# The value projection's first four slabs take ring places behind the down-projection's; the activation sum and the last norm's scales move

## The reference

```python
def swiglu(x, w_in, w_out):
    gate, up = jnp.split(x @ w_in, 2, axis=-1)
    return (jax.nn.silu(gate) * up) @ w_out
...
        h = layer_norm(DEEPNORM_ALPHA * h + y, ln_g[i, 0], ln_b[i, 0])
        h = layer_norm(DEEPNORM_ALPHA * h + swiglu(h, ffn_w_in[i], ffn_w_out[i]), ln_g[i, 1], ln_b[i, 1])
```

## Time and profile before

| | |
|---|---|
| median of 3 runs | 1138.2 us (1135.93 to 1138.34) |
| the profiled execution, its own time | 1138.06 us |
| its span, first to last instruction | 1136.2 us |
| mean granted TensorE clock | 0.997 |
| PE busy | 1122.7 us (99%) |
| DVE busy | 787.8 us (69%) |
| ACT busy | 570.1 us (50%) |
| POOL busy | 317.3 us (28%) |

### The profile page before, as it was taken

How to read it: one execution, slowest core, us unless ns; L and a number is a source line. 1 busy time by engine, 2 the same in 40 slices (tenths; PEclk the granted TensorE clock), 3 DMA queues, 4 the chain that set the end, 5 groups by cost and what they waited for, 6 DMA issues and landing times.

```text
span 1136.2 us, 18410 instructions
## 1 busy us (share of the span) xinstructions
PE 1122.7 (99%) x6828; PEld 996.3 (88%) x6828; DVE 787.8 (69%) x1266; ACT 570.1 (50%) x926; POOL 317.3 (28%) x212
## 2 busy tenths in 40 slices
PE   9999999999999999999999999999999999999997
PEld 7888888989999999888787877778989999997886
DVE  5070163798888885997603776766888888868987
ACT  4345144245555555556324665672435555556553
POOL 1538425141222212000155343551322222230001
PEclk9999999999999999999999999999999999999999
DMA  6433214076897755664232212142159879727551
GB/s 226 171 144 111 111 38 148 28 260 173 267 281 204 252 165 208 209 212 158 93 111 74 89 51 93 47 149 74 38 182 283 238 245 281 212 74 296 189 190 75
DMA packets 34459, 183.35 MB, mean 161 GB/s; under 512 B 3152, under 2 KB 7376, under 8 KB 20704
## 3 DMA queue, kind: packets, MB, share of 16 engines
q1 hardware_dynamic: 19472, 122.27, 29.9%
q0 software_dynamic: 8448, 46.14, 15.7%
q10 hardware_dynamic: 6480, 14.17, 3.5%
HBM read 180.46 MB, written 51.38 MB: 204 GB/s over the span
## 4 chain that ended last, share of the span: by engine, by line
PE 91%; DVE 3%; issue 2%; DMA 2%; ACT 1%; SPq 0%; DVEq 0%; POOL 0%; POOLq 0%; ACTq 0%
PE bank L2047 27%; PE bank L2049 27%; PE bank L2048 27%; PE bank L2499 2%; DVE s_w_lo L1321 2%; PE bank L2483 2%; DMA s_more_raw<-down 1%; PE bank L2130 1%; PE bank L2078 1%; PE bank L2520 1%; PE bank L2519 1%; DMA s_raw<-stream 1%; PE bank L2328 1%; PE bank L2321 0%; PE bank L2336 0%
## 5 line engine op out<-in xcount | busy, mean ns | idle before, releaser
L2047 PE MATMUL bank<-s_t_hi,s_w_hi 128*128 128x256 f32 (+1 forms) x832 | 264.4, 318 | 0.0
L2049 PE MATMUL bank<-s_t_hi,s_w_lo 128*128 128x256 f32 (+1 forms) x832 | 262.8, 316 | 0.0
L2048 PE MATMUL bank<-s_t_lo,s_w_hi 128*128 128x256 f32 (+1 forms) x832 | 262.8, 316 | 0.0
L1180 POOL TENSOR_TENSOR s_w_lo<-s_raw,s_w_hi 128x1024 fp32r<-128x1024 f32 x64 | 160.0, 2513 | 181.1 <-ACT s_w_hi L640 181.1
L640 ACT ACTIVATE s_w_hi<-s_raw 128x1024 fp32r<-128x1024 f32 x110 | 113.7, 1053 | 112.0 <-PE bank L2049 88.0
L2049 PEld LDWEIGHTS bank<-s_t_hi,s_w_lo 128*128 128x128 f32 x832 | 158.6, 191 | 10.2
L2047 PEld LDWEIGHTS bank<-s_t_hi,s_w_hi 128*128 128x128 f32 x832 | 158.7, 191 | 9.6 <-issue 0.2
L2048 PEld LDWEIGHTS bank<-s_t_lo,s_w_hi 128*128 128x128 f32 x832 | 158.7, 191 | 9.4
L1213 POOL TENSOR_TENSOR s_w_lo<-s_raw,s_w_hi 128x512 fp32r<-128x512 f32 x36 | 67.1, 1865 | 276.6 <-ACT s_w_hi L769 276.6
L2047 PE MATMUL bank<-s_t_hi,s_w_s_hi 128*128 128x256 f32 x432 | 122.4, 283 | 0.0
L2049 PE MATMUL bank<-s_t_hi,s_w_s_lo 128*128 128x256 f32 x432 | 122.2, 283 | 0.0
(11 more groups left out here) (248 smaller groups left out, 2483.3 us busy)
## 6 DMA issues: line engine op xcount, KB each, us to landing
s_raw<-stream SPq DMA_DIRECT2D x73, 1024.0 KB, 4.8
sums<-down POOLq DMA_DIRECT2D x12, 2816.0 KB, 20.9
sums<-sums POOLq DMA_DIRECT2D x4, 2816.0 KB, 13.2
s_more_raw<-sums SPq DMA_DIRECT2D x11, 1024.0 KB, 4.9
s_raw<-down SPq DMA_DIRECT2D x8, 1024.0 KB, 5.0
s_raw<-sums SPq DMA_DIRECT2D x5, 1024.0 KB, 4.9
s_ln_gb<-ln_gb ACTq DMA_DIRECT2D x4, 1024.0 KB, 7.1
s_more_raw<-down SPq DMA_DIRECT2D x4, 1024.0 KB, 6.9
```

The lines of the kernel that those rows point to most:

```text
L1180: nc.gpsimd.tensor_tensor(lo, raw_pair(SLOTS[place // 2])[:, n % 2, cols], hi.bitcast(F32), ALU.subtract).then_inc(lo_done, new)
L2047: nc.tensor.matmul(out, l_hi, r_hi, start=start, stop=False, skip_group_check=skip)
L2048: nc.tensor.matmul(out, l_hi, r_lo, start=False, stop=False, skip_group_check=skip)
L2049: return nc.tensor.matmul(out, l_lo, r_hi, start=False, stop=stop, skip_group_check=skip)
```

## The change

V0 to V3 leave the list of early slabs: they have no places of their own, are loaded and split behind the down-projection's slabs 36 to 39, and go to the ring places of these. Down-projection slabs 36 to 38 of the first layer load into `more_raw`, V0 to V3 into `raw`. The high halves of V0 and V1 stand on ACT between `turned_high(1)` and `square(2)`, those of V2 and V3 between `square(2)` and `square(3)`. The low halves of V0 and V1 are made by DVE, behind `turned_low(1)` and ahead of `centre(2)`; those of V2 and V3 by POOL, between the roots of tile 2 and tile 3. In the first layer `turned_low(1)` moves behind the means of tile 2.

In both layers `operand_sum(f, 2)` moves behind `low(8)`. In both the four merges of product 5 go tile by tile. In the last norm `scale` of tile 1 moves behind `centre` of tile 2, which gets a buffer of its own (`last_centred`), and the first term of the last mean moves behind the means of tile 2. `roots` is split into calls of `root`.

```diff
-EARLY = [FFN_IN[0], RPA_V, FFN_IN[1]]
+EARLY = [FFN_IN[0], FFN_IN[1]]
...
         early_places = {FFN_IN[0]: [(24, 28), (32, 36), (8, 12), (16, 20)],
-                        RPA_V: [(4, 12), (16, 20), (28, 32), (36, 40)],
                         FFN_IN[1]: [(32, 36), (40, 44), (76, 80), (68, 72)]}
...
         centred = sb_at("centred", [P, D_MODEL], F32, prod_at)
+
+        last_centred = sb_at("last_centred", [P, D_MODEL], F32, region)
...
                 if f is None:
-                    if slot >= RAWS:
-                        sp.wait_ge(slab_done, FFN_OUT[0])
                     sp.dma_start(raw_pair(slot), a["stream"][pair]).then_inc(raw_full[slot], 16)
                     continue
...
                 if early_of(n) is not None:
                     if n < RPA_V:
                         act.wait_ge(inter_done, TILES - 1)
-                    elif n < RPA_KQ:
-                        act.wait_ge(op_lo[0], lo_parts_until(PRODUCTS - 1, 1))
                     else:
...
                     if s == 35:
                         square(ln, 1)
                     split_hi(n0 + s)
-                if ln == 1:
-                    for j in range(TAIL):
-                        split_hi(n0 + DOWN + j)
                 for s in range(DOWN - TAIL, LAST_SLAB + 1):
                     split_hi(n0 + s)
                 if ln == 3:
@@ -731,7 +725,11 @@
                     return
                 turned_high(ln, 0, banks)
                 turned_high(ln, 1, banks)
+                split_hi(RPA_V)
+                split_hi(RPA_V + 1)
                 square(ln, 2)
+                split_hi(RPA_V + 2)
+                split_hi(RPA_V + 3)
                 square(ln, 3)
                 turned_high(ln, 2, banks)
                 turned_high(ln, 3, banks)
...
             feed_forward(0, FFN_IN[0])
-            roots(1)
+            root(1, 0)
+            root(1, 1)
+            root(1, 2)
+            pool.wait_ge(lo_done, RPA_V + 2)
+            for n in range(RPA_V + 2, RPA_V + TAIL):
+                split_lo(n)
+            root(1, 3)
             for n in range(RPA_V, RPA_KQ):
                 split_lo(n + RING)
...
-            def centre(ln, t):
+            def centred_of(ln, t):
+                return last_centred if (ln, t) == (3, 2) else centred
+
+            def centre(ln, t, behind=0):
 
                 if t == 0:
                     dve.wait_ge(gb_full, 16 * (ln + 1))
                 else:
-                    dve.wait_ge(normed[ln], t)
-                own(nc.vector.scalar_tensor_tensor(out=centred[:, :], in0=h[:, t, :], scalar=mean[:, t:t + 1],
+                    dve.wait_ge(normed[ln], t - behind)
+                own(nc.vector.scalar_tensor_tensor(out=centred_of(ln, t)[:, :], in0=h[:, t, :], scalar=mean[:, t:t + 1],
...
-                    nc.vector.scalar_tensor_tensor(out=h[:, t, cols], in0=centred[:, cols], scalar=rstd[:, t:t + 1],
+                    nc.vector.scalar_tensor_tensor(out=h[:, t, cols], in0=centred_of(ln, t)[:, cols], scalar=rstd[:, t:t + 1],
...
                 low(5)
                 operand_low(f, 1, 1)
                 low(6)
-                operand_sum(f, 2)
                 low(7)
                 low(8)
+                operand_sum(f, 2)
                 wait_product(dve, f, 0)
                 for t in early:
                     merge(f, 0, t, 0, first=True, minus=True)
...
                 scale(ln, 0)
                 low(35)
                 centre(ln, 1)
-                if ln == 1:
-                    for j in range(TAIL):
-                        split_low(n0 + DOWN + j)
                 for s in range(DOWN - TAIL, LAST_SLAB + 1):
                     low(s)
-                scale(ln, 1)
                 wait_product(dve, f, 5)
+                if ln == 1:
+                    scale(ln, 1)
                 for t in late:
                     merge(f, 5, t, 0, first=True, minus=True)
-                for t in late:
                     merge(f, 5, t, 1, last=True)
                 if ln == 1:
+                    dve.wait_ge(lo_done, RPA_V)
                     turned_low(ln, 0, banks)
-                    turned_low(ln, 1, banks)
                 dve.wait_ge(merged[f], 14)
-                if ln == 3:
-                    t = TILES - 1
-                    own(nc.vector.tensor_scalar(first_term[:, :], half_sum[:, t, 1:2], -ROOT_D / D_MODEL, ROOT_EPS,
-                                                ALU.mult, ALU.add))
                 dve.wait_ge(acc_done, TILES * (ln + 1))
                 merge(f, 6, 2, 0, last=True)
                 dve.wait_ge(merged[f], 15)
                 means(ln, 2)
-                centre(ln, 2)
-                scale(ln, 2)
-                dve.wait_ge(slab_done, n0 + DOWN)
                 t = TILES - 1
-                merge(f, 6, t, 0, last=True)
-                dve.wait_ge(merged[f], 16)
                 if ln == 1:
+                    turned_low(ln, 1, banks)
+                    split_low(RPA_V)
+                    split_low(RPA_V + 1)
+                    centre(ln, 2)
+                    scale(ln, 2)
+                    dve.wait_ge(slab_done, n0 + DOWN)
+                    merge(f, 6, t, 0, last=True)
+                    dve.wait_ge(merged[f], 16)
                     means(ln, t)
                     centre(ln, t)
                     scale(ln, t)
                     turned_low(ln, 2, banks)
                     turned_low(ln, 3, banks)
                     return
+                own(nc.vector.tensor_scalar(first_term[:, :], half_sum[:, t, 1:2], -ROOT_D / D_MODEL, ROOT_EPS,
+                                            ALU.mult, ALU.add))
+                centre(ln, 2, 1)
+                scale(ln, 1)
+                scale(ln, 2)
+                dve.wait_ge(slab_done, n0 + DOWN)
+                merge(f, 6, t, 0, last=True)
+                dve.wait_ge(merged[f], 16)
                 nc.vector.tensor_scalar(neg_mean[:, t:t + 1], half_sum[:, t, 0:1], -ROOT_D / D_MODEL, first_term[:, 0:1],
                                         ALU.mult, ALU.add).then_inc(mean_done, 1)
                 own(nc.vector.tensor_scalar(mean[:, t:t + 1], half_sum[:, t, 0:1], half_sum[:, t, 1:2], 1.0 / D_MODEL,
```

More of the change, by code:

```diff
@@ L1180, in split_lo, with root @@
                 nc.gpsimd.tensor_tensor(lo, raw_pair(SLOTS[place // 2])[:, n % 2, cols], hi.bitcast(F32), ALU.subtract).then_inc(lo_done, new)
+            def root(ln, t):
+                pool.wait_ge(squares, TILES * ln + t + 1)
+                if ln == 3 and t == TILES - 1:
+                    nc.gpsimd.tensor_tensor(rstd[:, t:t + 1], variance[:, t:t + 1], minus_half[:, 0:1], ALU.pow).then_inc(rstd_done, 1)
+                    return
+                own(nc.gpsimd.tensor_scalar(var_eps[:, t:t + 1], variance[:, t:t + 1], LN_EPS, None, ALU.add))
+                nc.gpsimd.tensor_tensor(rstd[:, t:t + 1], var_eps[:, t:t + 1], minus_half[:, 0:1], ALU.pow).then_inc(rstd_done, 1)
             def roots(ln):
                 for t in range(TILES):
-                    pool.wait_ge(squares, TILES * ln + t + 1)
-                    if ln == 3 and t == TILES - 1:
-                        nc.gpsimd.tensor_tensor(rstd[:, t:t + 1], variance[:, t:t + 1], minus_half[:, 0:1], ALU.pow).then_inc(rstd_done, 1)
-                        continue
-                    own(nc.gpsimd.tensor_scalar(var_eps[:, t:t + 1], variance[:, t:t + 1], LN_EPS, None, ALU.add))
-                    nc.gpsimd.tensor_tensor(rstd[:, t:t + 1], var_eps[:, t:t + 1], minus_half[:, 0:1], ALU.pow).then_inc(rstd_done, 1)
+                    root(ln, t)
             def out_projection(n0, ln):
```

## The result

| | before | after |
|---|---|---|
| median of 5 runs | 1138.01 us (1135.93 to 1138.34) | 1142.23 us (1142.01 to 1143.12) |
| span of the profiled execution | 1136.2 us | 1140.5 us |
| mean granted TensorE clock | 0.997 | 0.998 |
| PE's waits for lows: total, times, longest | 3.6, 3, 2.7 us | 4.2, 5, 1.4 us |

The changed kernel takes 1.0045 times as long, with a 95% interval of 1.0033 to 1.0057: slower, by 4.2 us. The forecast was 1142.5.

What follows compares the result with a forecast made beforehand. PE was taken as busy nearly throughout, losing time only in gaps, low clock or tail. Sum +4.4, ring places -0.4 and last norm +0.45 gave +4.4 on 1138.06: 1142.5 us, range 1138.0 to 1145.0.

Steps and rivals of the forecast that it cites:

- its four parts: Whole kernel: 2.2 in each layer's down-projection for the sum's move, -0.4 for the ring places, +0.45 for the last norm.
- Step 1, the sum: Both down-projections: the late sum holds operand_high(2) and split_hi(9) behind it; stops at slabs 9, 10, 12; +2.2 each, +4.4.
- the two old stops: PE's waits at slab 7, some 0.3 in the first layer's down-projection, 0.65 in the second's; -1.0 if they go.
- Step 2, the ring places: First layer's down-projection to tile 3's turn: long stop and low clock go, -4.65, but new stops leave only -0.4.
- the exclusion: VectorE operations with two SBUF inputs and GpSimd ones reading SBUF wait for each other's whole instruction, delaying scales, centres and roots.
- The terms for the tiles: New PE stops after the first layer's down-projection: 0.6 at V0, 1.4 at tile 2, 2.2 at tile 3.
- The undisturbed -3.7: Ring places by undisturbed durations: tile 3 turns at 558.2 against 561.92, -3.7 for the step.
- Step 3, the last norm: Last norm: root 2 is caught by centre(2), then scale(1); last merge at 1129.8, +0.45; without the exclusion -0.1.
- Undisturbed scales: Rival at 552 to 558: VectorE's scales don't wait for GpSimd; total +0.6, 1138.7 us; chance 0.18.
- a free sum: Rival: split_hi(9) isn't late or the sum's place doesn't hold it; -1.0 there, 1137.1 or 1133.2 us; chance 0.12.
- The clock didn't fall again: Rival: the clock falls in a new stop (1.4, 2.2 or 1.55), 1.75 each; 1144.2 or 1146 us; chance 0.15.
- the 1.75 of the prediction: Low clock (0.52) after the first layer's long down-projection stop: 1.75 of the 4.65 us lost there.

Runs made afterwards that it cites:

- the run with slab 9 first: Changed kernel, but ACT makes slab 9's high half before operand_high(2), the sum staying in its new place: 1138.04 us, 1.0002 times before.
- the last experiment: Kernel before with the sum between low(7) and low(8) and ACT's split of slab 9 ahead of operand_high(2): 1137.18 us, 0.9988 times before.
- the second set of edits: Four edits on the changed kernel: lows later on POOL 1146.82 us, last norm as before 1141.72, three repairs 1135.87, these with sum between low(7) and low(8) 1134.5.
- the three repairs: Changed kernel with slab 9 split before operand_high(2), lows of V2 and V3 on DVE, last norm as before: 1135.87 us, 0.9986 times before.

## Why the prediction was right

The sum was +4.4 and its four parts came out at +2.18, -0.83, +2.27 and +0.67, together 4.29. That the total is nearer than its parts is in part luck: the ring places gained 0.43 more than predicted, the last norm lost 0.22 more.

**Step 1, the sum.** Predicted 2.2 in each layer; the parts of the span are 2.18 and 2.27, the places of the stops alone 2.26 and 2.03. It is shown twice: taken back alone it gives 4.3, made alone it costs as much (4.6 between medians, 4.7 between spans, with a stop of 1.61 where the changed kernel has 1.40). The place of the loss was right too. By the starts the new stops were 1.52 and 1.67, 0.87 and 0.86, and 0.37 twice, where 1.55, 0.8 and 0.35 were worked out; the third, at slab 12, is too small for the list. The step that carried the forecast was to look at what stands behind `operand_high(2)` in ACT's queue; the run with slab 9 first shows that this queue, and not DVE's 3 us, held PE. One remark failed: that with slab 9 in time the two old stops would go as well (-1.0). 4.2 came back and not 5.2: small stops of 0.6 to 0.8 a layer stayed at slabs 10 and 12, which come from DVE's order behind the sum, and they weigh as much as the old ones. With the sum between low(7) and low(8) they are all but gone in the first layer: tile 0 turns 0.64 sooner (537.82 against 538.46).

**Step 2, the ring places.** Predicted -0.4, measured -0.83, and the same distance between the turns, 22.74 or 22.75, in the four kernels that have it in this form. The mechanism is shown: the exclusion was read off for other operations, and it holds for `scale` and `centre`, with 3.32 and 2.32 against 1.28. The rule of the Trainium skill (SBUF — State Buffer, Who interferes with whom) that whoever is issued first keeps the port to its end agrees with these rows, down to the order V2, `scale(2)`, V3, `centre(3)`. The terms for the tiles were too large: stops of 0.6, 1.4 and 2.2 were worked out; by the starts they were 0.7, 1.2 and 1.8 (the list has 0.43, 0.95 and 1.61). I had taken a low on POOL at 2.6, half of a pair of 5.23 that had itself been held up; alone it takes 2.40, a pair 4.67. The undisturbed -3.7 would have needed POOL's lows to run beside DVE for nothing; with the lows on DVE the turns are 20.61 apart instead of 23.57, a gain of 3.0. All these gains are against a profiled execution of the kernel before in which the clock fell (1.75). Where it didn't fall, the same ring places would lose some 0.9; that is an estimate, 1.75 - 0.83.

**Step 3, the last norm.** Predicted +0.45, measured +0.67. The exclusion is there, and what the order costs is 0.42, as worked out. The rest is the wait of 0.30 in front of `centre(2)`: from the merge's end at 1128.52 to `centre(2)` at 1129.38 it is 0.86, where the prediction had an estimate of 0.6 for the two means and the first term. Without that wait the same three take 0.60. Its cause is open (above).

**The rivals.** Undisturbed scales are refuted by the durations, a free sum by the two runs on the sum. The clock didn't fall again: it stood at 1.00 through the stops at slab 9 and those of 0.95 and 1.61.

## What to carry to other kernels

Moving work on one engine moves whatever another engine has queued for it, and everything behind that in the same queue: look for an instruction that needs nothing from the moved one and stands behind one that does, and reorder that queue in the same edit. Work given to POOL to relieve DVE cost nothing here only beside the merge, which reads PSUM; beside `scale` and `centre` the two engines' times add, so a low of 1.22 on DVE was cheaper than one of 2.40 on POOL. Before a transfer of work is put off, ask PE's order when it is first wanted, not when most of it is.

## What the hardware showed that I had not expected

**Tiny operations wait as long as large ones.** The root's two instructions work on 128 numbers and take 0.22 and 0.57. Beside a DVE operation of 1.2 us they took 1.32 and 1.52: they ended 0.1 and 0.4 after DVE's operation did.

**The same stop costs a varying amount.** The profiled executions with the long stop in layer 0 have the same 2.65 to 2.66 of idle PE, each behind the transposes of tile 0, but the clock stayed at its lower level (1.2 GHz) for different times: in the kernel before from 542, when PE had restarted, to the middle of 545; in the last experiment from 541, while PE was still idle, until after 547. By stretches of 1 us of that one:

```profile
542.00:543.00 1.00, 1.00 (x3) 0.73 (x3) 0.87 (x2) 0.00 (x0) 0.00 (x0) 0.50 0.00 0
...
547.00:548.00 1.00, 1.00 (x5) 0.72 (x4) 1.00 (x4) 0.00 (x0) 0.00 (x0) 0.62 1.03 434
548.00:549.00 1.00, 1.00 (x10) 1.00 (x9) 0.47 (x1) 0.40 (x1) 0.00 (x0) 1.00 1.02 434
```

The times show it too. Beside the second set of edits the kernel before lay in two groups, nine of 18 runs at 1136.34 to 1136.95 with a mean clock of 0.998 or 0.999 and nine at 1137.96 to 1138.57 with 0.997; the three repairs, which have no stop over 0.64, lay within 0.63 in eleven runs, at 0.998 and 0.999. That the lower group is the one where the clock didn't fall in that place, or only briefly, is an inference, since each kernel has one profiled execution. The size fits: 1.6 between the groups, against the 1.75 of the prediction and the 1.7 behind the stop of 4.93. If that is so, a stop that brings the clock down also widens the spread of the runs: 2.2 and 2.8 in the kernel before (18 and 27 runs), 0.6 to 1.3 in the kernels without it.
